# The eight sample rows of a decoder layer: split three-pass products replaced by plain fp32 products on four column strips

## What is computed

```python
q_a, kv_a, k_pe, glu_in, gate_logits = _split_in(u @ wts['w_in'])
# latents: 384 + 256 + 32 = 672 columns of w_in
q = einsum('btr,rhd->bthd', _rmsnorm(q_a, g_q_lat), w_uq)      # 16 heads x 96
q = _rmsnorm(concat(q[..., :64], _rope(q[..., 64:], pos)), g_q_head)
kv_lat, k_rope = _rmsnorm(kv_a, g_kv_lat), _rope(k_pe, pos)
k_nope = einsum('btl,lhd->bthd', kv_lat, w_uk)                 # 16 heads x 64
k = _rmsnorm(concat(k_nope, k_rope of every head), g_k_head)
v = einsum('btl,lhd->bthd', kv_lat, w_uv)
```

## Time and profile before

| | us |
|---|---|
| median of three runs (lowest, highest) | 1200.78 (1199.95, 1202.16) |
| profiled execution, its own time | 1201.45 |
| span of that execution, first to last instruction | 1199.4 |
| TensorE busy in it | 1159.5 (97%) |
| VectorE, ScalarE, GpSimd busy | 783.7, 589.8, 61.5 |

### The profile page before, as it was taken

How to read it: one execution, slowest core, us unless ns; L and a number is a source line. 1 busy time by engine, 2 the same in 40 slices (tenths; PEclk the granted TensorE clock), 3 DMA queues, 4 the chain that set the end, 5 groups by cost and what they waited for, 6 DMA issues and landing times.

```text
span 1199.4 us, 26051 instructions
## 1 busy us (share of the span) xinstructions
PE 1159.5 (97%) x9593; PEld 1107.2 (92%) x9593; DVE 783.7 (65%) x1304; ACT 589.8 (49%) x1149; POOL 61.5 (5%) x126
## 2 busy tenths in 40 slices
PE   6799999999999999999999999999999998999998
PEld 4699999989888899999999999999998998999998
DVE  1655554465675678888888888888766666555443
ACT  2454443345674665545545454554547354444432
POOL 1000000000000000101010101101010010000000
PEclk9799999999999999999999999999989999999999
DMA  9598658956435452021111202040236763655562
GB/s 330 197 306 280 187 175 301 351 166 167 129 108 205 106 145 61 16 65 36 46 54 25 74 12 73 25 125 1 64 107 217 250 183 103 185 182 184 167 188 68
DMA packets 162895, 169.84 MB, mean 142 GB/s; under 512 B 25614, under 2 KB 141073, under 8 KB 162791
## 3 DMA queue, kind: packets, MB, share of 16 engines
q1 hardware_dynamic: 162295, 167.88, 44.9%
q10 hardware_dynamic: 512, 0.82, 0.2%
HBM read 167.13 MB, written 2.49 MB: 141 GB/s over the span
## 4 chain that ended last, share of the span: by engine, by line
PE 87%; DVE 4%; ACT 3%; SPq 2%; DMA 2%; issue 2%; DVEq 0%; POOL 0%; ACTq 0%
PE PS L1683 25%; PE PS L1685 25%; PE PS L1684 25%; SPq L428 2%; PE PS L1742 2%; PE PS L2025 1%; PE PS L2050 1%; PE PS L2026 1%; DMA raw<-in_w_ffn_in 1%; DMA raw<-in_w_attn_out 1%; ACT wH L649 1%; PE PS L2021 1%; DVE oL L1609 1%; DVE wL L1054 0%; PE PS L1972 0%
## 5 line engine op out<-in xcount | busy, mean ns | idle before, releaser
L1054 DVE TENSOR_TENSOR wL<-raw,wH 128x1024 fp32r<-128x1024 f32 (+2 forms) x208 | 246.1, 1188 | 229.9 <-ACT wH L649 228.8
L649 ACT ACTIVATE wH<-raw 128x1024 fp32r<-128x1024 f32 (+2 forms) x208 | 213.4, 1029 | 269.6 <-PE PS L1685 248.4
L1683 PE MATMUL PS<-uH,wH 128*128 128x264 f32 x1024 | 295.7, 289 | 12.0 <-DVE uL L1105 8.5
L1684 PE MATMUL PS<-uL,wH 128*128 128x264 f32 x1024 | 293.3, 286 | 0.0
L1685 PE MATMUL PS<-uH,wL 128*128 128x264 f32 x1024 | 292.9, 286 | 0.0
L1683 PE MATMUL PS<-wqH,kTH 128*128 128x336 f32 (+2 forms) x768 | 255.3, 332 | 0.0
L1685 PE MATMUL PS<-wqH,kTL 128*128 128x336 f32 (+2 forms) x768 | 246.3, 321 | 0.0
L1684 PE MATMUL PS<-wqL,kTH 128*128 128x336 f32 (+2 forms) x768 | 245.9, 320 | 0.0
L1683 PEld LDWEIGHTS PS<-uH,wH 128*128 128x128 f32 x1024 | 195.5, 191 | 14.4 <-issue 9.9
L1684 PEld LDWEIGHTS PS<-uL,wH 128*128 128x128 f32 x1024 | 195.7, 191 | 0.1
L1685 PEld LDWEIGHTS PS<-uH,wL 128*128 128x128 f32 x1024 | 195.2, 191 | 0.0
(11 more groups left out here) (296 smaller groups left out, 1568.8 us busy)
## 6 DMA issues: line engine op xcount, KB each, us to landing
raw<-in_w_ffn_in SPq DMA_DIRECT2D x88, 512.0 KB, 3.6
adaw<-in_w_ada SPq DMA_DIRECT2D x72, 512.0 KB, 6.9
raw<-in_w_ffn_out SPq DMA_DIRECT2D x32, 512.0 KB, 3.6
raw<-in_w_in SPq DMA_DIRECT2D x32, 512.0 KB, 3.8
kv<-in_cache_kv_latent SPq DMA_DIRECT2D x128, 128.0 KB, 2.0
raw<-in_w_ffn_out SPq DMA_DIRECT2D x16, 384.0 KB, 3.1
raw<-in_w_attn_out SPq DMA_DIRECT2D x8, 512.0 KB, 6.7
raw<-in_w_conv_out SPq DMA_DIRECT2D x8, 512.0 KB, 3.6
```

The costliest lines, as they stand in the source:

```text
L649: f(wH[:, k, 0:width], raw[:, k, 0:width], ACT.Copy).then_inc(w_hi, 1)
L1054: v.tensor_tensor(wL[:, k, 0:width], raw[:, k, 0:width], wH[:, k, 0:width].bitcast(F32), ALU.subtract).then_inc(w_lo, 1)
L1683: mm(dst, a[0], b[0], start=start, stop=False)
L1684: mm(dst, a[0], b[1], start=False, stop=False)
```

## The change

For the eight sample rows, latents, keys and queries are no longer split in three. TensorE's array is used as four strips of 32 columns (`STRIPS`, helper `strips`): the stationary operand is the 8 rows in plain fp32, and each strip multiplies it by another quarter of the weight columns, taken from the loaded fp32 weights (`raw`, `wukF`), not from `wH` and `wL`.

- Latents: four matmuls of 168 columns per input block. Keys: eight of 256. Queries: twelve of 128 after every second chunk, with the stationary operand padded to 32 columns (`lqTn`).
- The results lie with strip `g` on partitions 32g to 32g+7. The latents are put back on 8 rows by four copies of VectorE (`lat_rows`). Keys and queries stay: four heads on each strip (`ktokS`, `qtokS`, `qnrow`, `qr4`), so that the samples' head work is done on 128 partitions with a quarter of the elements. The samples' queries are turned by 6 transposes of 128 x 128 in place of 24 small ones.
- Since TensorE now reads `raw`, loads into slots whose previous chunk is read so wait for `w_used` in place of `w_lo`: the second half of the latents' weights, the first GLU quad, all six query chunks, the third GLU quad.
- A query chunk is loaded by two DMAs of half the size with runs of 128 columns in place of one with runs of 256 (`query_chunk`), and its heads are dealt out so that a chunk has two strips' columns. A pair of query chunks is released together (`w_used` by 2 after the second).
- ScalarE takes squares in the order 0, 1, 2; the samples' wait for `lat_rows`. TensorE waits for `lat_rows` before `glu(0, 1)` where it waited for `lat_ready` 1.

The diff, cut to the parts that are spoken of:

```diff
-            def chunk(q, k, src, n_k, width, first=False):
+            def chunk(q, k, src, n_k, width, first=False, used=False):
 
                 if first:
                     sp.wait_ge(ada_used, 1)
+                elif used:
+                    sp.wait_ge(w_used, 4 * q + k - 3)
                 else:
                     sp.wait_ge(w_lo, 4 * q + k - 3)
...
-                    chunk(Q_QKV + i, k, win[:, 4 * i + k:4 * i + k + 1, 0:LAT], 1, LAT)
+                    chunk(Q_QKV + i, k, win[:, 4 * i + k:4 * i + k + 1, 0:LAT], 1, LAT, used=i > 0)
...
-                    chunk(Q_GLU[j], k, win[:, 4 * (k % 2):4 * (k % 2) + 4, col:col + 256], 4, 256)
...
+                    chunk(Q_GLU[j], k, win[:, 4 * (k % 2):4 * (k % 2) + 4, col:col + 256], 4, 256, used=j in (0, 2))
+
+            uq = x["w_uq"].rearrange("(k p) (g h) d -> p k g (h d)", p=P, g=4)
+
+            def query_chunk(n):
+
+                k = (n + 2) % 4
+                q = Q_UQV + (n + 2) // 4
+                sp.wait_ge(w_used, 4 * q + k - 3)
+                for m in range(2):
+                    sp.dma_start(raw[:, k, 0:768].rearrange("p (k g c) -> p k g c", k=3, g=2)[:, :, m, :],
+                                 uq[:, :, 2 * (n % 2) + m, P * (n // 2):P * (n // 2) + P]
+                                 ).then_inc(w_in[k] if m else uq_in[k], 16)
...
-            for t in (2, 0, 1):
+            for t in (0, 1, 2):
                 n = TILES[t][1]
                 own.wait()
-                f(junk[0:n, 0:QL], PS[0:n, 2 * t, 0:QL], ACT.Square, scale=QL ** -0.5,
-                  accum_out=ss6[0:n, 2 * t:2 * t + 1])
-                own.done(f(junk[0:n, 512:512 + KL], PS[0:n, 2 * t + 1, 0:KL], ACT.Square, scale=KL ** -0.5,
+                zq, zk = PS[0:n, 2 * t, 0:QL], PS[0:n, 2 * t + 1, 0:KL]
+                if t == 2:
+                    act.wait_ge(lat_rows, 4)
+                    zq, zk = lat[0:n, t, 0:QL], lat[0:n, t, QL:QL + KL]
+                f(junk[0:n, 0:QL], zq, ACT.Square, scale=QL ** -0.5, accum_out=ss6[0:n, 2 * t:2 * t + 1])
+                own.done(f(junk[0:n, 512:512 + KL], zk, ACT.Square, scale=KL ** -0.5,
                            accum_out=ss6[0:n, 2 * t + 1:2 * t + 2]))
             own.wait()
...
             def query_rows(p):
 
                 act.wait_ge(w_used, 4 * Q_UQV + 2 * p + 4)
-                for t in range(NT):
-                    m = TILES[t][1]
-                    i_ = f(qtok[0:m, t, :, :].rearrange("p h d -> p (h d)")[:, 512 * p:512 * p + 512],
-                           PS[0:m, UQ_BANKS[p][t], :], ACT.Copy)
-                i_.then_inc(use_act, 1)
+                for t in range(2):
+                    f(qtok[:, t, :, :].rearrange("p (g h) d -> p g (h d)", g=4)[:, :, P * p:P * p + P],
+                      PS[:, UQ_BANKS[p][t], :].rearrange("p (g c) -> p g c", g=4), ACT.Copy)
+                f(qtokS.rearrange("p h d -> p (h d)")[:, P * p:P * p + P], PS[:, UQ_BANKS[p][2], 0:P], ACT.Copy
+                  ).then_inc(use_act, 1)
...
@@ -1208,6 +1248,9 @@
             for i in range(8):
                 q, k = Q_QKV + i // 4, i % 4
                 ahead(q, k, LAT if q == Q_QKV else SLOT)
+            dve.wait_ge(w_used, 4 * Q_QKV + 8)
+            for g, a in enumerate(STRIPS):
+                v.tensor_copy(lat[0:NB, 2, LATQ * g:LATQ * g + LATQ], PS[a, 4, 0:LATQ]).then_inc(lat_rows, 1)
...
+                if i in (2, NT):
+                    z = hssS[:, :] if i == 2 else hss[:, i, 0:H // 4]
+                    own.done(v.tensor_reduce(z, junk[:, 0:H // 4 * QK].rearrange("p (h d) -> p h d", h=H // 4),
+                                             AX_X, ALU.add))
+                    own.wait()
+                    if i == 2:
+                        for g, a in enumerate(STRIPS):
+                            own.done(v.tensor_copy(hss[0:NB, i, 4 * g:4 * g + 4], hssS[a, :]))
+                        own.wait()
+                    dve.sem_inc(tok_root, 1)
+                    return
...
+            def strips(dst, a, parts, start, stop):
+
+                for g in range(4):
+                    i_ = mm(dst[QUAD * g:QUAD * g + a.shape[1], :], a, parts[g], start=start, stop=stop)
+                return i_
...
-                for t, (t0, n) in enumerate(TILES):
+                for t, (t0, n) in enumerate(TILES[0:2]):
                     a = (uH[:, kt, t0:t0 + n], uL[:, kt, t0:t0 + n])
                     product(PS[0:n, 2 * t, 0:QL], a, (wH[:, k, 0:QL], wL[:, k, 0:QL]), kt == 0, kt == KT - 1)
-                    i_ = product(PS[0:n, 2 * t + 1, 0:LAT - QL], a, (wH[:, k, QL:LAT], wL[:, k, QL:LAT]),
-                                 kt == 0, kt == KT - 1)
-                i_.then_inc(w_used, 1)
+                    product(PS[0:n, 2 * t + 1, 0:LAT - QL], a, (wH[:, k, QL:LAT], wL[:, k, QL:LAT]),
+                            kt == 0, kt == KT - 1)
+                strips(PS[:, 4, 0:LATQ], u[:, kt, SEQ:T],
+                       [raw[:, k, LATQ * g:LATQ * g + LATQ] for g in range(4)], kt == 0, kt == KT - 1
+                       ).then_inc(w_used, 1)
...
             pe.wait_ge(mod_turned, ADA_FFN)
             glu(0, 0)
-            pe.wait_ge(lat_ready, 1)
+            pe.wait_ge(lat_rows, 4)
             glu(0, 1)
...
                 if t == 2:
                     pe.wait_ge(g_free, G_GLU + 4)
-                for c in range(2):
+                    for kt in range(2):
+                        i_ = strips(PS[:, 4, 0:256], kvTn[:, kt, :],
+                                    [wukF[:, kt, 256 * g:256 * g + 256] for g in range(4)], kt == 0, kt == 1)
+                for c in range(2 if t < 2 else 0):
...
-                for t, (t0, n) in enumerate(TILES):
+                for t, (t0, n) in enumerate(TILES[0:2]):
                     bank, c0 = UQ_BANKS[n_ // 2][t], 256 * (n_ % 2)
                     for kt in range(3):
-                        i_ = product(PS[0:n, bank, c0:c0 + 256], (latH[:, kt, t0:t0 + n], latL[:, kt, t0:t0 + n]),
-                                     (wH[:, k, 256 * kt:256 * kt + 256], wL[:, k, 256 * kt:256 * kt + 256]),
-                                     kt == 0, kt == 2)
-                i_.then_inc(w_used, 1)
+                        product(PS[0:n, bank, c0:c0 + 256], (latH[:, kt, t0:t0 + n], latL[:, kt, t0:t0 + n]),
+                                (wH[:, k, 256 * kt:256 * kt + 256], wL[:, k, 256 * kt:256 * kt + 256]),
+                                kt == 0, kt == 2)
+                for kt in range(3 if n_ % 2 else 0):
+                    i_ = strips(PS[:, UQ_BANKS[n_ // 2][2], 0:P], lqTn[:, kt, :],
+                                [raw[:, k - 1 + m, 256 * kt + P * e:256 * kt + P * e + P]
+                                 for m in range(2) for e in range(2)], kt == 0, kt == 2)
+                if n_ % 2:
+                    i_.then_inc(w_used, 2)
...
-            for j in range(H // 2):
-                tr(PS[:, 4, NB * j:NB * j + NB], qnrow[:, 2 * j:2 * j + 2, :].rearrange("p a d -> p (a d)"), ident[0:NB, 0:NB])
-            for hd in range(H):
-                i_ = tr(PS[:, 4, 64 + NB * hd:64 + NB * hd + NB],
-                        qr4[:, hd, :, :].rearrange("p r d -> p (r d)"), ident[0:NB, 0:NB])
+            for j in range(2):
+                tr(PS[:, 4, P * j:P * j + P], qnrow[:, 2 * j:2 * j + 2, :].rearrange("p a d -> p (a d)"), ident)
+            for hd in range(H // 4):
+                i_ = tr(PS[:, 5, P * hd:P * hd + P], qr4[:, hd, :, :].rearrange("p r d -> p (r d)"), ident)
```

More of the change, by code:

```diff
@@ L74 @@
 QUAD = 32
+STRIPS = [slice(QUAD * g, QUAD * g + NB) for g in range(4)]
+LATQ = LAT // 4
 SUMMED = (4, 5, 3)
@@ L1334, in _ @@
                 "p (a n) -> p a n", a=2)))
+            own.done(v.tensor_copy(lqTn[:, :, 0:NB], PS[:, LAT_BANK + 2, SEQ:SEQ + 3 * NB].rearrange(
+                "p (a n) -> p a n", a=3)))
             own.done(v.tensor_copy(krTn[:, :], PS[0:ROPE, LAT_BANK + 2, SEQ + 5 * NB:SEQ + 6 * NB]))
```

96 lines of the change are left out of this document (65 added, 31 removed).

## The result

The changed kernel took **1206.19 us** (median of 20 runs, 1200.8 to 1210.2) beside 1202.03 for the kernel before (20 runs, 1199.95 to 1205.8): ratio on record 1.0029, 95% interval 1.0018 to 1.0041 (the two medians by themselves give 1.0035). Slower by 0.3%; forecast was 1197.5, range 1194.3 to 1201.5. Run again it had 1.0039 (1.0026 to 1.0052) and 1.0022 (1.0007 to 1.0037). The profiled execution had a span of 1202.6 and an own time of 1204.43.

The account below looks back on a forecast made before the run. TensorE, busy for 97% of the span, was taken as the bound. The terms -3.5 + 1.15 - 0.1 - 0.85 = -3.3 took 1201.45 to 1198.15, and the runs' median 0.7 lower gave 1197.5 us, range 1194.3 to 1201.5.

Parts of the forecast that it names:

- From E to K: End of the latents to start of the keys: late fourth GLU chunk and sample-row copies delay the latents' turn, +1.15 us.
- E: Clock point: the end of the latents on TensorE, when the last copy starts, 285.05 us in the kernel before.
- K: Clock point: the start of the keys, 310.4 us in the kernel before.
- Latents, -3.5: Latents' input blocks: strips replace a third of each block's matmuls, saving 3.5 us (bounds 2.3 and 5).
- The cover of 1.5 us: In the latents, later loads of blocks 4 to 7 are ready 5.5 us after release, needed after 7.0.
- From K to G, -0.1: Keys, queries and turns: nearly all that keys and queries give (1.8 and 3.8 us) is waited away, leaving -0.1.
- G: Clock point: the start of `glu(2, 0)`, 350.87 us in the kernel before.
- Behind G, -0.85: After `glu(2, 0)` starts: six 128x128 turns take 0.75 us where 24 small ones took 1.64, -0.85.
- late loads in series: Rival: four serial loads from latents to turns; each 1.7 us later gives 1204.3, slower from +0.85 each; 9%.
- The clock, at 17%: Rival: idle pieces before `glu(2, 0)` bring a further 3.4 us at 1.2 GHz, costing 1.7: 1199.2 us; 17%.
- Strips in turn: Rival: strips in latents, keys and queries do not run side by side, 12.5 us more on TensorE: 1206; 2%.
- absent waits: Rival: ScalarE and VectorE run further ahead, so keys and queries give half or all their 5.6 us: 1194.7 or 1192; 13%.

Follow-up runs that it names:

- the second profile: The changed kernel run once more, unaltered, and profiled again; its median was 1205.64 us, beside 1201.09 for the kernel before.

## Why the prediction was wrong

- **The step that failed** is "From E to K. ... It lands at E+3.8, ... +1.15." Measured +3.8, +7.1 and +7.0. Of it, by the chain: landing at E+4.6 to E+6.8 in place of E+3.8; the four copies 0.35 each in place of 0.24; and the stretch at 1.2 GHz over `glu(0, 1)`, 1.2 to 2.5, which this step put at nothing. The median of 3.8 in the earlier trace rows hides a spread: in the same trace four loads of 512 KB issued 0.5 apart (427.2 to 428.8) landed in 3.8, 4.8, 5.9 and 6.9. And the prediction did not look at what stood behind the held-back loads on SP's queue, where w_uk's 1 MB lay; what that alone costs in time was not told apart from the noise. The Trainium skill, "DMA: Bandwidth & Descriptors", Anatomy of one DMA, has 2.0 us plus bytes over 436 GB/s, an estimate of 3.2 for this chunk. That section is on DMAs issued by GpSimd, and these are issued by SyncE; the trace of the kernel before has 3.6 at best for a 512 KB load of `w_in` (3.3 for any of that size), and the late chunk took 4.1 to 6.8 in the kernels with strips.
- **Latents, -3.5:** -2.7 at equal clock. The group is 0.47 long as drawn, but a block shrank by 0.31, not 0.42: the matmuls on both sides of a group stand further apart too, so it costs 0.6, which lay inside the bounds of 0.30 to 0.65. The rest, down to -4.1 in the second profile, is a stretch at 1.2 GHz that was absent there, which is luck. The cover of 1.5 us for the loads of blocks 4 to 7 held: the groups stay 2.45 apart.
- **From K to G, -0.1** (its own steps give 40.3 - 40.5 = -0.2): +1.7, +1.5 and +1.2. The steps were right in kind and order: samples' keys 1.05 as forecast, waits of 1.0 and 1.1 for values and first queries (forecast 0.7 and 0.9), waits of 1.8 and 2.5 in the turns (forecast 1.4 and 2.6), end of the queries to G 11.3 (11.1). What was missing is 0.5 in the first two of these waits, 0.4 ahead of the samples' keys, 0.3 in each of three query pairs (16.12 / 3 = 5.4 in place of 5.1) and, in the first profile, 32 turns in 5.45 us, partly at 1.2 GHz.
- **Behind G, -0.85:** the samples' turns fell as said (from their start to that of `qabs` 13.4 before, 12.4 now). Then the small matmuls of `qabs` met one stretch more at 1.2 GHz and took that back: 4.82 us for 64 where they had 3.69. In the other two profiles the stage was 1.3 longer than before, with the clock at 1.2 GHz for 10 us of it.
- **The rivals.** The first, late loads in series, at 9%, is the nearest, but it asked for four loads that each land later (turning point +0.85 a load): the first landed 0.8 to 3.0 later than forecast, the other three within 0.5. The clock, at 17%, did fall, with three to four stretches of 3.4 us more between E and the first scores: over all runs the mean granted clock is 0.981 to 0.982 against 0.983 to 0.987. "TensorE: Matmul & The Clock Gate", Part 1 (the Trainium skill), has idleness bring the throttle back, and the rows agree (0.99 in the window of the wait, 0.50 and 0.51 in the two behind it); but holding the clock did not give the time back here. Strips in turn (2%) and absent waits (13%) are both excluded by the rows above.
- **The mark set beforehand** was "`glu(0, 1)` about 1.2 after `glu(0, 0)`, turns of the latents at E+13.2". It showed the error at once: 2.3 and E+16.0 by the chain.

The sum with what was measured, against the profile before: -3.2 + 6.0 + 1.5 + 0.9, and 0.4 behind the scores, gives +5.6, the mean difference of the three spans; the medians of the runs had +4.2, +4.5 and +3.4.

## What to carry to other kernels

When an edit makes a buffer's release later, price not that load alone but everything that stands behind it: on the issuing queue, on the engine that copies it, and behind that copy in program order. An instruction that waits for a DMA should stand behind the evictions that TensorE waits for: that reordering was worth 0.5% in each of two stages (in the latents together with w_uk's load put first), as much as all the arithmetic that the strips save. An experiment that moves one wait has to be read for the wait that comes in its place, in this case twice. And a duration on which the sum rests should be taken from more than one execution where a DMA is in it.
